# A fused mixer and MLP block in Strassen form: Up's results stored in three pieces, raw Down weights loaded behind them, copies and block loads moved

## The reference

```python
def mixer_sublayer(x, norm_g, w_in, ..., w_out):
    h = rms_norm(x, norm_g)
    z = h @ w_in
    ...
    return x + jnp.concatenate([ya, yr, yp], axis=-1) @ w_out

def mlp_sublayer(x, norm_g, w_up, w_down):          # w_up 1024 x 4096, w_down 4096 x 1024
    h = rms_norm(x, norm_g)
    return x + jnp.square(jax.nn.relu(h @ w_up)) @ w_down

def reference(x, ...):
    x = mixer_sublayer(x, ...)
    x = mlp_sublayer(x, ...)
    return rms_norm(x, final_norm_g)
```

## Time and profile before

| what | value |
|---|---|
| median of 3 runs | 2241.41 us |
| profiled execution, its own time | 2244.33 us |
| its span in the profile | 2242.1 us |
| mean granted TensorE clock | 0.977 of full |
| TensorE matmul busy | 2084.7 us (93%) |
| VectorE busy | 1316.5 us (59%) |
| ScalarE busy | 926.2 us (41%) |
| GpSimd busy | 477.8 us (21%) |

### The profile page before, as it was taken

The page is one execution under the profiler, slowest core; times in us unless marked ns, Lnnn a source line. Parts: engine busy times, 40 slices in busy tenths (PEclk is TensorE's granted clock), DMA queues, the critical chain, the costliest instruction groups (busy, mean ns, idle before and its releaser), DMA issues.

```text
span 2242.1 us, 28085 instructions
## 1 busy us (share of the span) xinstructions
PE 2084.7 (93%) x10172; PEld 1744.7 (78%) x10172; DVE 1316.5 (59%) x1864; ACT 926.2 (41%) x1581; POOL 477.8 (21%) x387
## 2 busy tenths in 40 slices
PE   8998999899989988798899698897999999999998
PEld 6987798789878976577778486676878888888887
DVE  3347345633563466877777877675654455645455
ACT  4443343344344423533454543443533334433333
POOL 6256425542644463200000300000000000000001
PEclk9999999999999998899999899999999999999999
DMA  7122421241133221379877378877694554864452
GB/s 261 58 84 90 151 67 66 100 151 57 66 135 115 85 104 66 97 220 227 238 166 179 91 194 222 223 190 202 155 328 188 191 199 181 319 236 188 188 195 106
DMA packets 114883, 357.51 MB, mean 159 GB/s; under 512 B 10011, under 2 KB 11836, under 8 KB 100412
## 3 DMA queue, kind: packets, MB, share of 16 engines
q1 hardware_dynamic: 110140, 338.93, 48.4%
q10 hardware_dynamic: 4608, 16.78, 2.0%
HBM read 262.22 MB, written 93.45 MB: 159 GB/s over the span
## 4 chain that ended last, share of the span: by engine, by line
PE 43%; DVE 6%; DMA 4%; issue 3%; ACT 2%; SPq 1%; POOL 0%; DVEq 0%; ACTq 0%; POOLq 0%
PE bank L1803 14%; PE bank L1804 14%; PE bank L1805 14%; DMA wraw<-in_wup 1%; DMA d_raw<-in_wdn 1%; DMA u_dram<-ur 1%; DVE wt L1555 1%; DVE wraw L1555 1%; DVE ur L1590 1%; DVE ur L1607 0%; DVE ur L1605 0%; DVE ua L1574 0%; ACT tA L1073 0%; ACT ur L1079 0%; DVE ur L1600 0%
## 5 line engine op out<-in xcount | busy, mean ns | idle before, releaser
L1803 PE MATMUL bank<-h_hi,w_lo 128*128 128x512 f32 x896 | 360.0, 402 | 91.4 <-ACT tA L1073 71.3
L1804 PE MATMUL bank<-h_lo,w_hi 128*128 128x512 f32 x896 | 355.2, 396 | 0.0
L1805 PE MATMUL bank<-h_hi,w_hi 128*128 128x512 f32 x896 | 354.6, 396 | 0.0
L1803 PE MATMUL bank<-d_hi,u_lo 128*128 128x512 f32 x896 | 348.9, 389 | 3.0 <-DVE d_lo L1709 3.0
L1804 PE MATMUL bank<-d_lo,u_hi 128*128 128x512 f32 x896 | 348.6, 389 | 0.0
L1805 PE MATMUL bank<-d_hi,u_hi 128*128 128x512 f32 x896 | 348.6, 389 | 0.0
L661 POOL TENSOR_TENSOR ring_lo<-stage,ring_hi 128x1024 fp32r<-128x1024 f32 x104 | 246.8, 2396 | 306.0 <-ACT ring_hi L823 305.8
L1709 DVE TENSOR_TENSOR u_lo<-u_raw,u_hi 128x1024 fp32r<-128x1024 f32 x112 | 137.1, 1224 | 270.8 <-ACT u_hi L1107 270.8
L1803 PEld LDWEIGHTS bank<-h_hi,w_lo 128*128 128x128 f32 x896 | 172.2, 192 | 141.7 <-DVE w_lo L1563 79.2
L1107 ACT ACTIVATE u_hi<-u_raw 128x1024 fp32r<-128x1024 f32 x112 | 118.5, 1058 | 342.4 <-PE bank L1805 326.3
L1803 PE MATMUL bank<-ring_hi,hT_lo 128*128 128x384 f32 (+1 forms) x672 | 246.8, 367 | 0.1
(11 more groups left out here) (185 smaller groups left out, 3425.6 us busy)
## 6 DMA issues: line engine op xcount, KB each, us to landing
u_raw<-u_dram SPq DMA_DIRECT2D x56, 1024.0 KB, 4.8
stage<-in_wmix SPq DMA_DIRECT2D x108, 512.0 KB, 3.4
u_dram<-ur SPq DMA_DIRECT2D x32, 1536.0 KB, 12.8
wraw<-in_wup SPq DMA_DIRECT2D x128, 256.0 KB, 4.1
d_raw<-t_dram SPq DMA_DIRECT2D x32, 1024.0 KB, 7.0
d_raw<-in_wdn SPq DMA_DIRECT2D x24, 1024.0 KB, 8.4
traw<-in_wdn SPq DMA_DIRECT2D x16, 1024.0 KB, 6.7
t_dram<-traw SPq DMA_DIRECT2D x16, 1024.0 KB, 5.0
```

The source lines that it names most:

```text
L1803: pe.matmul(dst, al, bh, start=(first and k == 0), stop=False, skip_group_check=chain)
L1804: pe.matmul(dst, ah, bl, start=False, stop=False, skip_group_check=chain)
L1805: last = pe.matmul(dst, ah, bh, start=False, stop=(final and k == n - 1), skip_group_check=chain)
```

## The change

`store_u` makes three DMAs: `ua` as before; `ur`'s first block as soon as ScalarE has squared it (semaphore `ub_stored`); the other five blocks after `combine_end`. `combine(n, 3)` waits for `ub_stored` in place of `ur_stored`. `load_t` stands behind `store_u` in a pair, and `t_sums` behind `combine(n, 3)`. In the turn, ScalarE makes `h_high(1, 5)` after the pair's first copy and not before it, and `h_high(1, 6)` after `relu_square(n, 0)`. The four DMAs of Down's steps 0 and 1 are issued one each in pairs 26, 27, 28 and 29.

```diff
@@ store_u
                 sp.wait_ge(r_done, 6 * n + 2)
                 sp.dma_start(u_dram[p, 0, j // GP, :, j % GP, :], ua[n % 2][:, :]).then_inc(ua_stored[n % 2], 16)
+                sp.wait_ge(r_done, 6 * n + 4)
+                sp.dma_start(u_dram[p, 1, j // GP, :, j % GP, :], ur[:, 0, :]).then_inc(ub_stored, 16)
                 sp.wait_ge(c_done, 10 * n + 10)
-                sp.dma_start(u_dram[p, 1:7, j // GP, :, j % GP, :].rearrange("k p t -> p k t"), ur[:, :, :]).then_inc(ur_stored, 16)
+                sp.dma_start(u_dram[p, 2:7, j // GP, :, j % GP, :].rearrange("k p t -> p k t"), ur[:, 1:6, :]).then_inc(ur_stored, 16)
@@ the loop of SyncE (load_step is split into load_step_u and load_step_d)
                     load_w(n + 1, B12)
-                if n in T_PAIRS:
-                    load_t(T_PAIRS.index(n))
                 if 7 <= n < 15:
                     load_h(1, n - 7)
                 if n:
                     store_u(n - 1)
+                if n in T_PAIRS:
+                    load_t(T_PAIRS.index(n))
@@
                     sp.wait_ge(t_stored, 16 * len(T_PAIRS))
-                    load_step(0)
-                    load_step(1)
+                    load_step_u(0)
+                if n == 27:
+                    load_step_d(0)
+                if n == 28:
+                    load_step_u(1)
+                if n == 29:
+                    load_step_d(1)
@@ ScalarE
                 relu_22(n - 1)
-                if n == NPAIR:
-                    h_high(1, 5)
                 w_high(n, 6)
                 square_22(n - 1)
@@
                 if n == NPAIR:
-                    h_high(1, 6)
+                    h_high(1, 5)
                 chain_out(n, 1)
                 relu_square(n, 0)
+                if n == NPAIR:
+                    h_high(1, 6)
@@ VectorE, combine(n, 3)
                     dve.wait_ge(prod_done, NK * n + 6)
-                    dve.wait_ge(ur_stored, 16 * n)
+                    dve.wait_ge(ub_stored, 16 * n)
@@
-                if n in T_PAIRS:
-                    t_sums(T_PAIRS.index(n))
                 if 7 <= n < 15:
                     h_norm(1, n - 7)
                 combine(n, 2)
@@
                 combine(n, 3)
+                if n in T_PAIRS:
+                    t_sums(T_PAIRS.index(n))
                 if more:
                     w_low(n + 1, 5)
```

More of the change, by code:

```diff
@@ L343, in build @@
         ua_stored = [sem(f"ua_stored{s}") for s in range(2)]
+        ub_stored = sem("ub_stored")
         ur_stored = sem("ur_stored")
@@ L543, in store_t, with load_step_u @@
                 sp.dma_start(t_dram[i // GP, :, :, i % GP, :].rearrange("r p n -> p r n"), traw[:, :, :]).then_inc(t_stored, 16)
-            def load_step(s):
+            def load_step_u(s):
                 p, k, g = step_of(s)
@@ L552, in load_step, with load_step_d @@
                 sp.wait_ge(ua_stored[1], 8 * n)
+                sp.wait_ge(ub_stored, 16 * n)
                 sp.wait_ge(ur_stored, 16 * n)
                 sp.dma_start(u_raw[s % RAW][:, :, :], u_dram[p, k, g]).then_inc(u_full[s % RAW], 16)
+            def load_step_d(s):
+                p, k, g = step_of(s)
+                if s >= RAW:
+                    sp.wait_ge(m_lo_done, 4 * (s - RAW) + 4)
                 if k in (0, 1, 5):
@@ L560, in load_step @@
                 sp.dma_start(d_raw[s % RAW][:, :, :], src).then_inc(d_full[s % RAW], 16)
+            def load_step(s):
+                load_step_u(s)
+                load_step_d(s)
             for i in range(5):
```

## The result

The changed kernel takes **2253.85 us** (median of 4 runs, 2253.59 to 2255.28) against 2240.04 for the kernel before beside it: a ratio of 1.0069, 95% interval 1.0055 to 1.0083. It is slower by 13.8 us, where I had forecast 2219.1. The profiled execution took 2253.71, its span is 2251.5.

The account below looks back on a forecast made before the run. TensorE is busy 93% of the span, so only its idle time and slow clock can be won. Pair 27 -13.2, turn -4.5, raw-weight pairs -4.6: -22.3 from 2241.4 gives 2219.1 us; forecast's range 2209 to 2233, 8 in 10 2204 to 2236.

Parts of the forecast that it names:

- the store rate r: Pairs with raw weights: the stores of ua and ur run at 190 GB/s, so 1.83 MB take 9.6 us.
- the period of 22.0 us: Pairs with raw weights: one round from t_sums to t_sums takes 22.0 us; both passes together -4.6 us.
- The lead before the first X: First pass: the first t_sums ends 21.0 us after the start of pair 1.
- The tail: First pass, after the last t_sums: B12 lands 6.8 later, product 4 starts 3.5 behind, three products 8.2, transposes 0.9.
- the clock's loss comes off the next stall: Pairs with raw weights: the longer stall may cost clock, but the next stall shrinks by it; no size given.
- rival 2: Pairs with raw weights: stores at 155 GB/s make a period of 24.2, slower at 2250 us; chance 0.05.
- Order of events: Pairs with raw weights: VectorE idles before t_sums until traw lands, one stall before product 4, none before product 2.
- The period of today: Pairs with raw weights: the new 22.0 us equals today's period, same bytes and VectorE work in another order.
- The old circle: Kernel before, raw-weight pairs: ur store 14.5 us, then combine(n, 3) to the next ur store 8.1, together 22.6.
- Pair 27: One load ahead of B12 in place of four: -13.2 of 13.4 us, bounds -11 and -13.4.
- The turn: Pair 16: product 4 comes 5.9 us earlier, product 6 is next late; -4.5 us, between -3 and -5.
- Rival 1: Pairs free of stalls if stores exceed 275 GB/s, the circle under TensorE's 19.04: -68, 2174 us; chance 0.08.

Follow-up runs that it names:

- the combination: Changed kernel with raw weights in their old places, u_dram's planes 1 MiB apart, grow loaded in pair 25, h_high(1, 6) one step further ahead: 2174.4 us.
- The part alone: Kernel before with only the load and sums of the raw weights moved as in the change: 2268.0 us, ratio 1.0128.

## Why the prediction was wrong

**The step that failed is the store rate r in the pairs with raw weights, and with it the period of 22.0 us.** I took 190 GB/s, between 181 and 205 of the earlier trace rows, because no `traw` is read as the stores begin. Term by term in pair 3, from X = 978.3, the end of `t_sums`:

| term | sum | measured |
|---|---|---|
| to `t_dram`'s issue | 1.1 | 1.0 |
| `t_dram` lands | 5.0 | 5.6 |
| B12 behind it | 0.7 | 0.7 |
| the stores of `ua` and `ur` | 9.6 | 11.3 |
| `traw` | 2.7 | 2.2 |
| `t_sums` | 2.9 | 2.9 |
| period | 22.0 | 23.6 |

11.3 us for 1.83 MB are 162 GB/s. That no `traw` was read beside them did not make the stores faster: they are limited by themselves. The kernel before could have told me. In the pair of the 181 row (1012.50 to 1017.50) `traw` had been issued at 1004.85 and landed 6.6 us later, before the row begins, so 181 was already a rate without it:

```profile
1004.85 0.38 SPq L539 DMA_DIRECT2D traw<-in_wdn  x1
```
```profile
traw<-in_wdn SPq DMA_DIRECT2D x1, 1024.0 KB, 6.6
```

Seven periods of the first pass run from 954.40 to 1124.90, 170.5 us, where seven of 22.0 and the two `hx` loads made 156.8: the five without `hx` average 23.6, the two with it 26.3, so an `hx` load cost 2.7 and not 1.4. The lead before the first X is 23.2 instead of 21.0. The tail is 21.5 instead of 19.4, 1.6 of it three products at a granted clock of 0.84: 10.7 us from product 4 where I had 8.2 and 0.9. That is 13.7 + 2.2 + 2.1 = 18.0, the whole difference from 197.2 to 215.2. I had written that the clock's loss comes off the next stall; in the tail there is no next stall. The second pass missed by 13.4, of which 12.6 are its seven periods of 23.8 (`t_sums` begins at 1326.56 for the first time and at 1493.12 for the last).

This is rival 2, at 155 GB/s, 24.2 a period and 2250, to which I gave 0.05. I held against it that it needs a rate below all three rows. But by my own sums the change costs time from a period of 23.6 on, and the row of 160 gives 23.8: that row alone, a store without raw weights beside it, put the kernel at 2244, outside my range, which stopped at a period of 23.0. Three rows from 160 to 205 for one kind of transfer were a spread to carry into the range, since 14 us of result hang on each microsecond of period. What lies beyond 2244 is the rest of the sum: the `hx` loads, the lead and the tail, pair 27 and the turn.

- **Order of events: right.** VectorE idles at `t_sums` until `traw` lands (37.9 us in 16 waits), one stall before product 4, none before product 2. `traw` landed 15.2 us after the store's issue (13.4 in the sum), and `ur` 2.4 us before `relu_22` (996.85 and 999.28).
- **"The period of today": wrong.** The old circle had neither `t_dram`'s store nor `t_sums` in it. The new one has both, in series with the stores of `ua` and `ur` and the load. The part alone costs 28 us on the kernel before; at a period of 22.0 it would have cost next to nothing.
- **Pair 27: right in kind**, -10.8 of -13.2. The wait that is left is VectorE's 3.52 us for B12, of which I had 0.2; TensorE stalls for 2.3 of it. My sum counted `grow` by its bytes, 1.4 us. In this trace its issue alone holds SyncE for 1.74 us (0.43 to 1.68 in those of the other kernels), `u_raw` goes out 1.55 us after the pair's end, and behind `grow` it takes 7.5 us where I had 5.0. With `grow` a pair earlier, in the combination, TensorE's stall is 0.1 us. The queue, as timeline:

```profile
1533.75 1.74 SPq L599 DMA_DIRECT2D grow<-in_gfin  x1
1535.73 0.33 SPq L558 DMA_DIRECT2D u_raw<-u_dram  x1
1536.24 0.33 SPq L526 DMA_DIRECT2D wraw<-in_wup  x1
```

- **The turn: right up to product 4** (27.9 us after its start, 28.0 in the sum). GpSimd took 7.34 us for its four and not the 6.4 of the sum, so product 6 came at 37.0 and not 36.2, and then ran at a granted clock of 0.61, 4.43 us for 2.72: -2.5 instead of -4.5. (Product 6 at 1291.2 for 1296.2 is -5.0; the forecast took -4.5, between its bounds, and names no term for the half.)

```profile
1296.34 7.34 POOL L809 TENSOR_TENSOR h_lo<-hraw,h_hi 128x512 fp32r<-128x512 f32 x4 [22.87 <-ACT h_hi L1074]
```

- **Rival 1 had the right mechanism at the wrong place.** Above 275 GB/s the circle falls under TensorE's period, I wrote, and no row shows such a rate. With another step between the planes the store goes at 383, and the changed kernel takes 2192.8. There `traw` is late once, by 1.3 us, but B12 behind `t_dram`'s store still makes VectorE wait, 28.2 us in all, so it stays above the 2174 of the combination. The combination has what rival 1 describes, pairs free of stalls (49 us less), pair 27 (13.0 less) and 2.7 of the turn, but it needed the raw weights back in front for it.

In sum: 18.0 and 13.4 in the pairs, 2.4 in pair 27 and 2.0 at the turn make 35.8 of the 36.1 between -22.3 and +13.8.

## What to carry to other kernels

When a load is moved behind a slow store, ask what waits for the load, and write down the whole new circle with every transfer in series: what used to run beside the store now adds to it. If the period of that circle is a term of the forecast, the rate of its largest transfer has to be known to a few per cent, and its lowest row is a candidate like the others. And a transfer that keeps all DMA engines busy at half the rate of another with equal rows is itself the thing to mend first: here the order of a tensor's axes was worth 50 us, more than every reordering that worked around it.

## What the runs showed of the hardware

A store of five planes of 256 KB, rows of 2 KB, took 11.9 us (median) with planes 4 MiB apart and 6.6 to 7.2 with 5, 2 or 1 MiB; in pairs without raw weights 180 against 383 GB/s, with the DMA engines' share at 1.0 both times. The page DMA: Bandwidth & Descriptors of the Trainium skill (Latency and other measured facts) tells of copies whose rows in HBM lie a large power of two apart: 164 GB/s at 2 MiB and 103 at 4 MiB, and full speed with 4 KiB more. Here the rows within a plane lie close and it is the planes that are far apart. The runs agree that 4 MiB is slow and a step of 5 MiB, no power of two, is not; they differ at 2 MiB, where planes lose nothing. That the planes' rows then fall on the same part of the memory is a guess; no run looked at it.
